# A three-block transformer pass: the fourth mixer's latent query scaling, a key turn and four insertions moved

## The chip, the cores and the metric

One NeuronCore of a Trainium2 chip runs the whole program in one launch. Its engines work side by side and meet only by semaphores: PE multiplies matrices, DVE (vector) and ACT (scalar) work on elements, POOL (GpSimd) does a few small ones, SP issues the DMAs. The metric is the device time of one execution in microseconds; the kernel before takes 1460.8 us (median of 3 runs, 1460.72 to 1460.99).

## The reference

256 rows of 1024 features pass through two layers of a first block (feed-forward, mixer, feed-forward), then one layer of a second block. The "fourth mixer" of this text is the mixer of the second block. It runs two attentions of 8 heads beside each other, "fox" with forget gates and "latent" (MLA), and adds them under sigmoid gates:

```
proj = h @ w_in[l]
(q_lat, kv_lat, k_rope, fq, fk, fv, f_logit, g_mla, g_fox) = jnp.split(proj, split_points, axis=-1)
y_mla = mla_mixer(q_lat, kv_lat, k_rope, cos, sin, ...)   # q, k: 64 normalised + 32 rotated columns
y_fox = fox_mixer(fq, fk, fv, f_logit, ...)               # q, k: 64 normalised columns, decay from f_logit
mixed = (jax.nn.sigmoid(g_mla + b_gate[l, 0]) * (y_mla @ w_branch_mla[l])
         + jax.nn.sigmoid(g_fox + b_gate[l, 1]) * (y_fox @ w_branch_fox[l]))
x = x + mixed @ w_o[l]
```

In `mla_mixer` the queries come from `rms_norm(q_lat) @ w_qb`. Each head's 64 plain and 32 rotary columns are normalised apart, and the rotary ones are then rotated by position. The rotated key (32 columns, from `k_rope`) is the same for all heads. Both attentions are causal softmax(q k) v.

## The kernel before, in words

Every float32 weight matrix is streamed from HBM and multiplied in three passes. The weights lie in blocks of at most 512 rows by 512 columns (1 MB), in the order of the list `plan`. For each block SP loads it into one of 4 slots of `raw`; ACT casts it to a high part `whi` (line 1193); DVE subtracts to get a low part `wlo` (line 1632); PE multiplies high by high, low by high and high by low (lines 563 to 565). `whi` and `wlo` have 3 slots each. A cast waits until PE is done with the block three places before, a load until DVE has made the low part of the block four places before. In the programs of ACT and DVE `unit()` is the cast or the low part of the next block; both run a few blocks ahead of PE.

`steps(job, i, j0, j1)` is PE's work on row tiles j0 to j1 of block i of a job: per row tile two halves of the rows and three matmuls each. A full block has 4 row tiles, 24 matmuls. Before each matmul group it waits for the low part of the block:

```
q.wait_ge(*s_dve[job.key, kt])
q.wait_ge(*s_lo[v, j])
```

In the mixers these blocks are one piece each: `s_lo` is raised once, when the whole low part is done.

Each engine's program is one list, written out by hand and executed in order. PE's list sets insertions between `steps` of the gate blocks (`gate2[0]` to `gate2[3]`, each with two blocks, 0 and 1): the attention's transposes, scores and values, which need results of ACT, DVE and POOL. PE's PSUM is handed out as 4 pairs of banks in a ring (`take`, `give`); a pair comes free when ACT or DVE has read it.

The insertions, of PE unless named otherwise:

- `fox_turn(g)`: transposes of 4 heads of fox queries and keys (line 1018); ACT copies them to `mQT`, `mKT` (line 1480).
- `fox_scores(g)`: matmuls q k of 4 heads (line 717). DVE's `logits` adds the causal mask and takes maxima (lines 1893, 1896), ACT's `softmax` the exponentials (line 1324), DVE's `normalise` divides (lines 1904, 1906).
- `probabilities(mat, ("f", g), g)`: transposes of the probabilities (lines 730 to 736), copied by ACT (line 1336) and DVE (line 1914).
- `fox_values(g)`: matmuls p v (lines 750, 751), read out by `turned` on ACT and DVE.
- `rope_key_turn()`: two transposes of the rotated key, which POOL makes (lines 2342 to 2260, `s_pool["kr", 1]`); ACT copies it to all heads (line 1549).
- `mla_queries(g)`, `mla_keys()`, `mla_scores(g)`: the same for the latent attention (lines 1010, 1018, 717; ACT lines 1486, 1492).

The latent queries' norm factors come from DVE's `head_factors("q")`; `head_scale("q")` multiplies them in, 4 instructions (line 2106). Then POOL rotates the rotary columns (lines 2349, 2258, 2260), and PE's `mla_queries(0)` waits for that (`s_pool["qrope", 1]`).

In DVE's list the order around the change is: low part of `kvb[1]` (512 columns, small); `head_scale("q")`; low part of `gate2[0]`, block 1; logits of both fox groups; `normalise` of the first; low part of `gate2[1]`, block 0; copy of probabilities; `gate(0)`; `normalise` of the second; low part of `gate2[1]`, block 1. In ACT's list the copy of the rotated key stands behind the cast of `gate2[3]`, block 0.

Of the kernel before, what the change touches and what calls it, by code (L numbers as in the profile page):

```python
# [183 lines left out]
def bc(ap, dim, n):  # L184
    a = ap.unsqueeze(dim)
    shape = list(a.shape)
    shape[dim] = n
    return a.broadcast_to(shape)


def program(nc, T, out):
    with ExitStack() as ctx:
# [341 lines left out]
        def tensor(e):  # L534
            q = Waits(e)
            idle = [(0, ()), (1, ()), (2, ()), (3, ())]

            def take(name):
                i, emptied = idle.pop(0)
                for mark in emptied:  # L540
                    q.wait_ge(*mark)
                pair_of[name] = i
                return Pair(name)

            def give(name, *emptied):
                idle.append((pair_of[name], emptied))

            def steps(job, i, j0=0, j1=4):
                v = job.at[i]
                k0, nk, _ = job.blocks[i]  # L550
                pair = take(job.name) if i == 0 and j0 == 0 else Pair(job.name)
                wd, end = job.width, i == len(job.blocks) - 1
                order = [(j, tt) for j in range(j0, min(j1, nk)) for tt in range(2)]
                if v == len(plan) - 1:
                    return last_steps(job, pair, v, k0, nk)
                for j, tt in order:
                    kt, n = k0 // 128 + j + job.k_off, job.rows(i, j)
                    q.wait_ge(*s_dve[job.key, kt])
                    q.wait_ge(*s_lo[v, j])
                    hi_w, lo_w = (w[0:n, v % SPLIT, j * wd:(j + 1) * wd] for w in (whi, wlo))  # L560
                    h, l = (a[0:n, kt, 128 * tt:128 * tt + 128] for a in (job.act.hi, job.act.lo))
                    o = pair.ap[:, tt, 0:wd]
                    e.matmul(o, h, hi_w, start=i == 0 and j == 0, stop=False)  # L563
                    e.matmul(o, h, lo_w, start=False, stop=False)  # L564
                    t = e.matmul(o, l, hi_w, start=False, stop=(end or (v == len(plan) - 2 and tt == 1)) and j == nk - 1)  # L565
                    if j == nk - 1:
                        t.then_inc(s_mm.mark((v, tt), *([(job.name, tt)] if end else [])), 1)

            def last_steps(job, pair, v, k0, nk):

                wd, own = job.width, take("last")
                for tt, c0, n in ((0, 0, wd), (1, 0, wd // 2), (1, wd // 2, wd // 2)):
                    o = own.ap[:, c0 // (wd // 2), 0:n] if tt else pair.ap[:, 0, :]
                    for j in range(nk):
                        kt = k0 // 128 + j + job.k_off
                        q.wait_ge(*s_dve[job.key, kt])
                        q.wait_ge(*s_lo[v, j])
                        hi_w, lo_w = (w[:, v % SPLIT, j * wd + c0:j * wd + c0 + n] for w in (whi, wlo))
                        h, l = (a[:, kt, 128 * tt:128 * tt + 128] for a in (job.act.hi, job.act.lo))
                        e.matmul(o, h, hi_w, start=tt == 1 and j == 0, stop=False)  # L580
                        e.matmul(o, h, lo_w, start=False, stop=False)
                        t = e.matmul(o, l, hi_w, start=False, stop=j == nk - 1)
                    names = [("last", tt, c0)]
                    if c0 + n == wd:
                        names += [(v, tt), (job.name, tt)]
                    t.then_inc(s_mm.mark(*names), 1)
# [407 lines left out]
            def mla():  # L994
# [26 lines left out]
                def fox_turn(g):  # L1021
                    pair = take(("fx", g))
                    q.wait_ge(*s_pool["hn", "fq"])
                    two_heads(pair, 0, ("fxq", g), FQ, g)
                    q.wait_ge(*s_dve["hn", "fk"])
                    two_heads(pair, 1, ("fxk", g), FK, g)
                    give(("fx", g), s_act["fxk", g])
# [7 lines left out]
                def fox_values(g):  # L1035
                    q.wait_ge(*s_act["fv"])
                    values(mat, ("f", g), lambda h, st: FV[:, st, 64 * (4 * g + h):64 * (4 * g + h) + 64], 64, ("yt", "fox"), 4 + 2 * g)

                def rope_key_turn():
                    pair = take("krt")  # L1040
                    q.wait_ge(*s_pool["kr", 1])
                    for tt in range(2):
                        t = e.transpose(pair.ap[0:96, 0, 128 * tt:128 * tt + 128], KR[:, tt, :], ident[:, :])
                    t.then_inc(s_turn.mark("krt"), 1)
                    give("krt", s_act["krt"])
# [42 lines left out]
                steps(kvb[0], 0)  # L1088
                give(kvb[0].name, s_act["kv", 0])
                fox_turn(0)  # L1090
                steps(gate2[0], 0, 0, 2)
                fox_turn(1)
                steps(gate2[0], 0, 2, 3)
                fox_scores(0)
                steps(gate2[0], 0, 3)
                fox_scores(1)
# [3 lines left out]
                probabilities(mat, ("f", 0), 0)  # L1100
                give(gate2[0].name, s_dve["gate", 0])
                steps(gate2[1], 0)
                fox_values(0)
                steps(gate2[1], 1, 0, 2)
                probabilities(mat, ("f", 1), 1)
                steps(gate2[1], 1, 2, 3)
                fox_values(1)
                steps(gate2[1], 1, 3)
                give(gate2[1].name, s_dve["gate", 1])
                steps(gate2[2], 0, 0, 1)  # L1110
                rope_key_turn()
                mla_queries(0)
                mla_keys()
                steps(gate2[2], 0, 1, 3)
# [58 lines left out]
            ffn(b2)  # L1173
            ffn(c1)
            mla()
            ffn(c2)

        def scalar(e):
            q = Waits(e)
            at_unit = [0]  # L1180

            def unit():
                v = at_unit[0]
                at_unit[0] += 1
                if v < len(plan):
                    for js, n, c in pieces(v):
                        high(v, js, n, c)
# [274 lines left out]
            def mla():  # L1462
# [20 lines left out]
                def mla_queries(g):  # L1483
                    q.wait_ge(*s_turn["m_", "s", ("f", 1), 0])
                    q.wait_ge(*s_turn["mq", g])
                    e.mul(mQT[:, 4 * g:4 * g + 4, :], Pair(("mq", g)).flat[0:96, :].rearrange("p (h t) -> p h t", h=4),
                          96.0 ** -0.5).then_inc(s_act.mark(("mq", g)), 1)
# [55 lines left out]
                probabilities(mat, ("f", 1), ("f", 0))  # L1543
                unit()
                turned(("m_", "v", ("f", 1)), YT, 6, None, (128,) * 2)
                unit()
                q.wait_ge(*s_turn["m_", "s", ("f", 1), 0])
                q.wait_ge(*s_turn["krt"])
                e.copy(mKT[64:96, :, :], bc(Pair("krt").ap[64:96, 0, 0:256], 1, 8)).then_inc(s_act.mark("krt"), 1)
                mla_queries(0)  # L1550
                mla_keys(0)
                mla_keys(1)
# [57 lines left out]
        def vector(e):  # L1610
            q = Waits(e)
# [3 lines left out]
            def after_mine():  # L1615
                q.wait_ge(*s_dve.now())

            def unit():
                v = at_unit[0]
                at_unit[0] += 1  # L1620
                if v < len(plan):
                    ps_ = pieces(v)
                    for p in ps_:
                        low(v, *p, done=p is ps_[-1])
# [274 lines left out]
            def normalise(at, g, i):  # L1899
                name = at.name  # L1900
                for tt in (1, 0):
                    L, c = at.part(i, tt)
                    q.wait_ge(*s_act[name, "exp", g, tt])
                    e.reciprocal(at.ri[:, c:c + 4], at.sm[:, c:c + 4]).then_inc(s_dve.mark(), 1)
                    after_mine()
                    e.tensor_tensor(L, L, at.ri[:, c:c + 4].unsqueeze(2).broadcast_to([128, 4, 128 * (tt + 1)]),
                                    ALU.mult).then_inc(s_dve.mark((name, "P", g, tt)), 1)
# [173 lines left out]
            def mla():  # L2081
# [20 lines left out]
                def head_scale(name):  # L2102
                    views = norm_views[name]
                    after_mine()
                    for i, x in enumerate(views):
                        t = e.tensor_tensor(x, x, r24[:, 8 * i:8 * i + 8].unsqueeze(2).broadcast_to([128, 8, x.shape[2]]), ALU.mult)
                        t.then_inc(s_dve.mark(*([("hn", name)] if i == len(views) - 1 else [])), 1)
# [44 lines left out]
                head_sums("q", (2, 3))  # L2152
                head_factors("q")
                unit()
                head_scale("q")
                unit()
                logits(mat, ("f", 0), 0, causal)
                logits(mat, ("f", 1), 1, causal, ("fxk", 1))
                normalise(mat, ("f", 0), 0)
                unit()  # L2160
                q.wait_ge(*s_pool["kr", 1])
                probabilities(mat, ("f", 0))
# [250 lines left out]
```

## Time and profile before

| | |
|---|---|
| median of 3 runs | 1460.8 us (1460.72 to 1460.99) |
| span of the profiled execution, first to last instruction | 1458.9 us |
| PE busy | 1452.6 us |
| DVE, ACT, POOL busy | 1002.6, 778.5, 87.2 us |
| all waits of PE for another engine | 3.4 us |

The span is the profiled execution's own time. It leaves out what lies before the first and behind the last instruction, so it stands 1.9 us below the runs' median. Times inside it are in us from its start; the fourth mixer lies at about 1110 to 1290. A row of a timeline gives start, duration, engine, line, operation, output and inputs, and count, and in brackets the idle time ahead of it with the engine that ended it. Matmul ends are modelled and overlap, so PE's rows are read by their starts.

### The profile page before, as it was taken

To read this page: it belongs to the slowest core of one execution; us is meant where nothing else is said; L and a number is where in the kernel's file an instruction comes from. 1 tells how busy PE (TensorE), PEld (TensorE's weight loads), DVE (VectorE), ACT (ScalarE), POOL (GpSimd) and SP (SyncE) were. 2 spreads that over 40 slices of the span, in tenths; PEclk is the share of its full clock that TensorE was granted. 3 is DMA by queue.
4 is the path that set the end of the run, shared out by engine and by line. 5 is a ranking of instruction groups with operands and counts; after the bars stand their busy time and mean duration, and the time that the engine had idled before them with its cause. 6 is when DMAs were issued, how large, how long until landed. Compare 5 with 4: busy or idle time off the path is not lost.

```text
span 1458.9 us, 18627 instructions
## 1 busy us (share of the span) xinstructions
PE 1452.6 (100%) x7822; PEld 1250.3 (86%) x7822; DVE 1002.6 (69%) x1216; ACT 778.5 (53%) x971; POOL 87.2 (6%) x113
## 2 busy tenths in 40 slices
PE   9999999999999999999999999999999999999999
PEld 7888888888888888888888888888888888888887
DVE  6976466787755867459877664787646987687653
ACT  6654355655534555345665544564435876465542
POOL 0000003000000000006100000000000800000000
PEclk9999999999999999999999999999999999999999
DMA  9855563556556555545455556475556543556552
GB/s 328 277 183 178 160 203 116 168 180 201 179 182 202 187 187 189 186 139 172 150 198 188 189 172 206 154 223 182 187 173 217 188 144 118 173 193 205 178 187 72
DMA packets 205620, 266.82 MB, mean 183 GB/s; under 512 B 6944, under 2 KB 148880, under 8 KB 205280
## 3 DMA queue, kind: packets, MB, share of 16 engines
q1 hardware_dynamic: 204320, 261.23, 54.5%
q0 software_dynamic: 1072, 4.35, 0.8%
q8 instruction: 62, 1.02, 0.3%
q14 instruction: 22, 0.18, 0.0%
q10 hardware_dynamic: 144, 0.05, 0.0%
HBM read 264.56 MB, written 1.05 MB: 182 GB/s over the span
## 4 chain that ended last, share of the span: by engine, by line
PE 96%; DVE 2%; ACT 1%; DMA 0%; issue 0%; DVEq 0%; ACTq 0%
PE ps L637 33%; PE ps L643 17%; PE ps L563 14%; PE ps L565 13%; PE ps L564 13%; PE ps L616 1%; PE ps L717 1%; PE ps L812 1%; DVE wlo L1632 1%; PE ps L750 1%; DVE d_i L2025 0%; DVE d_m L2021 0%; DMA G<-in_gains 0%; DVE d_i L2049 0%; PE ps L751 0%
## 5 line engine op out<-in xcount | busy, mean ns | idle before, releaser
L1632 DVE TENSOR_TENSOR wlo<-raw,whi 128x2048 fp32r<-128x2048 f32 (+5 forms) x275 | 567.4, 2068 | 259.0 <-ACT whi L1193 258.6
L1193 ACT CAST whi<-raw 128x2048 fp32r<-128x2048 f32 (+5 forms) x275 | 474.7, 1732 | 222.8 <-PE ps L565 218.4
L637 PE MATMUL ps<-xt,whi 128*128 128x512 f32 x2112 | 511.2, 391 | 0.5 <-DVE xt L2225 0.5
L637 PEld LDWEIGHTS ps<-xt,whi 128*128 128x128 f32 x2112 | 386.0, 188 | 74.4 <-DVE xt L2225 1.3
L643 PEld LDWEIGHTS ps<-xt,wlo 128*128 128x128 f32 x2112 | 274.0, 191 | 12.3
L643 PE MATMUL ps<-xt,wlo 128*128 128x256 f32 x2112 | 277.7, 283 | 0.0
L563 PE MATMUL ps<-whi,xt 128*128 128x512 f32 (+4 forms) x304 | 112.7, 371 | 0.0
L565 PE MATMUL ps<-whi,xt 128*128 128x512 f32 (+4 forms) x304 | 109.7, 361 | 0.0
L564 PE MATMUL ps<-wlo,xt 128*128 128x512 f32 (+4 forms) x304 | 109.5, 360 | 0.0
L563 PEld LDWEIGHTS ps<-whi,xt 128*128 128x128 f32 x304 | 57.3, 188 | 9.2 <-issue 1.0
L565 PEld LDWEIGHTS ps<-whi,xt 128*128 128x128 f32 x304 | 57.2, 188 | 8.5
L564 PEld LDWEIGHTS ps<-wlo,xt 128*128 128x128 f32 x304 | 57.4, 189 | 7.4
L1206 ACT ACTIVATE xt<-ps,G 128x256 fp32r<-128x256 f32 x64 | 25.1, 474 | 35.6 <-PE ps L616 35.5
L563 PE MATMUL ps<-whi,yt_hi 128*128 128x512 f32 (+3 forms) x108 | 42.7, 395 | 0.0
L565 PE MATMUL ps<-whi,yt_lo 128*128 128x512 f32 (+3 forms) x108 | 41.7, 386 | 0.0
L564 PE MATMUL ps<-wlo,yt_hi 128*128 128x512 f32 (+3 forms) x108 | 41.6, 386 | 0.0
L1222 ACT ACTIVATE junk<-X 128x512 f32<-128x512 f32 x40 | 25.4, 634 | 28.5 <-DVE X L1690 27.3
L1646 DVE SCALAR_TENSOR_TENSOR xt<-ps,G,xt 128x256 fp32r<-128x256 f32 x64 | 26.5, 477 | 15.6 <-ACT xt L1206 15.6
L563 PE MATMUL ps<-whi,a1ht_hi 128*128 128x512 f32 x88 | 34.3, 390 | 0.0
L563 PE MATMUL ps<-whi,a2ht_hi 128*128 128x512 f32 x88 | 34.3, 390 | 0.0
L563 PE MATMUL ps<-whi,b1ht_hi 128*128 128x512 f32 x88 | 34.3, 390 | 0.0
L563 PE MATMUL ps<-whi,b2ht_hi 128*128 128x512 f32 x88 | 34.3, 390 | 0.0
(422 smaller groups left out, 1885.8 us busy)
## 6 DMA issues: line engine op xcount, KB each, us to landing
raw<-in_ffn_wi SPq DMA_DIRECT2D x85, 1024.0 KB, 4.9
raw<-in_ffn_wo SPq DMA_DIRECT2D x40, 1024.0 KB, 5.0
raw<-in_ffn_w_gate SPq DMA_DIRECT2D x22, 1024.0 KB, 5.1
raw<-in_ffn_w_up SPq DMA_DIRECT2D x22, 1024.0 KB, 5.2
raw<-in_ffn_w_down SPq DMA_DIRECT2D x20, 1024.0 KB, 4.9
raw<-in_w_in SPq DMA_DIRECT2D x14, 1024.0 KB, 5.1
raw<-in_even_w_in SPq DMA_DIRECT2D x6, 1024.0 KB, 5.2
raw<-in_ffn_wo SPq DMA_DIRECT2D x8, 512.0 KB, 3.8
```

Source lines behind the costliest of these rows:

```text
L563: e.matmul(o, h, hi_w, start=i == 0 and j == 0, stop=False)
L564: e.matmul(o, h, lo_w, start=False, stop=False)
L565: t = e.matmul(o, l, hi_w, start=False, stop=(end or (v == len(plan) - 2 and tt == 1)) and j == nk - 1)
L616: t = e.transpose(pair.flat[0:n, 256 * b + 128 * tt:256 * b + 128 * tt + 128], halves[tt], ident[:, :])
L637: return e.matmul(pair.ap[:, b, :], whi[:, v % SPLIT, 256 * j + 128 * b:256 * j + 128 * b + 128], XS[:, j, :, :].rearrange("p h t -> p (h ...
L643: e.matmul(pair.ap[:, b, 0:256], wlo[:, v % SPLIT, 256 * j + 128 * b:256 * j + 128 * b + 128], XS[:, j, 0, :], start=False, stop=False)
L717: t = e.matmul(pair.flat[:, w * h:w * h + w], queries(h)[0:n, 128 * tt:128 * tt + 128], keys(h)[0:n, 0:w], start=True, stop=True)
L1193: e.copy(whi[0:n, v % SPLIT, c], raw[0:n, v % RAW, c]).then_inc(s_hi.mark(*[(v, j) for j in js]), 1)
L1206: t = e.mul(act.hi[0:n, kt0 + i, :], pair.flat[0:n, 256 * i:256 * i + 256], 1.0 if gains is None else gains(i)[0:n, :])
L1222: e.activation(junk[:, :], X[:, tt, 512 * n:512 * n + 512], ACT.Square, accum_out=ssq[:, tt, n:n + 1]).then_inc(s_act.mark(("sq", x, n, tt ...
L1632: e.tensor_tensor(wlo[0:n, v % SPLIT, c], raw[0:n, v % RAW, c], whi[0:n, v % SPLIT, c].bitcast(F32), ALU.subtract).then_inc(s_lo.mark(*[(v ...
L1646: t = e.scalar_tensor_tensor(l, src, gains(i)[0:n, :], h.bitcast(F32), ALU.mult, ALU.subtract)
```

## The change

Four moves, in the programs of PE, ACT and DVE; no instruction is added or taken away.

- PE: the second fox turn follows the first directly, and the first three row tiles of `gate2[0]`, block 0, come behind both.
- PE: one row tile of `gate2[1]`, block 1, comes ahead of the first fox values, which are then followed directly by the second fox probabilities; the next two row tiles come behind these.
- PE and ACT: the rotated key's turn moves from `gate2[2]` to behind the second fox values, and ACT's copy of it to before the cast of `gate2[3]`, block 0.
- DVE: `head_scale("q")` moves from ahead of the low part of `gate2[0]`, block 1, to behind `normalise` of the first fox group.

```diff
@@ tensor, mla
                 fox_turn(0)
-                steps(gate2[0], 0, 0, 2)
                 fox_turn(1)
-                steps(gate2[0], 0, 2, 3)
+                steps(gate2[0], 0, 0, 3)
                 fox_scores(0)
                 steps(gate2[0], 0, 3)
                 fox_scores(1)
...
                 steps(gate2[1], 0)
+                steps(gate2[1], 1, 0, 1)
                 fox_values(0)
-                steps(gate2[1], 1, 0, 2)
                 probabilities(mat, ("f", 1), 1)
-                steps(gate2[1], 1, 2, 3)
+                steps(gate2[1], 1, 1, 3)
                 fox_values(1)
+                rope_key_turn()
                 steps(gate2[1], 1, 3)
                 give(gate2[1].name, s_dve["gate", 1])
                 steps(gate2[2], 0, 0, 1)
-                rope_key_turn()
                 mla_queries(0)
@@ scalar, mla
                 turned(("m_", "v", ("f", 1)), YT, 6, None, (128,) * 2)
-                unit()
                 q.wait_ge(*s_turn["m_", "s", ("f", 1), 0])
                 q.wait_ge(*s_turn["krt"])
                 e.copy(mKT[64:96, :, :], bc(Pair("krt").ap[64:96, 0, 0:256], 1, 8)).then_inc(s_act.mark("krt"), 1)
+                unit()
                 mla_queries(0)
@@ vector, mla
                 head_factors("q")
                 unit()
-                head_scale("q")
                 unit()
                 logits(mat, ("f", 0), 0, causal)
                 logits(mat, ("f", 1), 1, causal, ("fxk", 1))
                 normalise(mat, ("f", 0), 0)
+                head_scale("q")
                 unit()
```

## Rows read from the trace of the kernel before

**Rows 1.** The page, busy time by engine (us, share, instructions).
```profile
PE 1452.6 (100%) x7822; PEld 1250.3 (86%) x7822; DVE 1002.6 (69%) x1216; ACT 778.5 (53%) x971; POOL 87.2 (6%) x113
```
**Rows 2.** PE's waits, whole span: total us, times, longest.
```profile
...
PE ps L717 <- DVE m_L L1893: 0.7, 1, 0.7
...
PE ps L717 <- ACT m_kt L1492: 0.2, 1, 0.2
```
**Rows 3.** The chain of waits, 1157 to 1197 us: start, us, what.
```profile
1157.53 2.06 DVE m_qf L2106 x4
...
1191.83 1.87 ACT m_kt L1549
...
1195.33 0.70 ACT m_kt L1492
```
**Rows 4.** DVE's timeline, 1157 to 1199 us.
```profile
1157.44 2.14 DVE L2106 TENSOR_TENSOR m_qf<-m_qf,m_r 128x512 f32<-128x512 f32 x4
1159.51 2.30 DVE L1632 TENSOR_TENSOR wlo<-raw,whi 128x2048 fp32r<-128x2048 f32 x1
1161.73 1.21 DVE L1893 SCALAR_TENSOR_TENSOR m_L<-causal,ps 128x1024 f32<-128x1024 f32 x1
...
1171.28 2.28 DVE L1632 TENSOR_TENSOR wlo<-raw,whi 128x2048 fp32r<-128x2048 f32 x1
...
1177.56 2.29 DVE L1632 TENSOR_TENSOR wlo<-raw,whi 128x2048 fp32r<-128x2048 f32 x1
...
1198.10 1.22 DVE L1893 SCALAR_TENSOR_TENSOR m_L<-causal,ps 128x1024 f32<-128x1024 f32 x1 [2.45 <-PE ps L717]
```
**Rows 5.** ACT's timeline, 1151 to 1192 us.
```profile
1151.17 1.27 ACT L1230 ACTIVATE m_fv<-ps,RS 128x512 f32<-128x512 f32 x2 [0.76 <-PE ps L565]
...
1156.19 2.42 ACT L1193 CAST whi<-raw 128x512 fp32r<-128x512 f32 x2
...
1159.86 1.38 ACT L1480 ACTIVATE m_kt<-ps,G 64x512 f32<-64x512 f32 x2
...
1189.89 1.92 ACT L1193 CAST whi<-raw 128x2048 fp32r<-128x2048 f32 x1 [0.98 <-PE ps L565]
```
**Rows 6.** PE's timeline, 1158 to 1197 us.
```profile
1158.21 2.78 PE L717 MATMUL ps<-m_kt,m_qt 80*128 80x256 f32 x16
...
1163.08 2.86 PE L717 MATMUL ps<-m_kt,m_qt 80*128 80x256 f32 x16 [0.70 <-DVE m_L L1893]
...
1173.82 0.48 PE L563 MATMUL ps<-whi,xt 128*128 128x512 f32 x1
...
1179.16 0.39 PE L565 MATMUL ps<-whi,xt 128*128 128x512 f32 x1
1179.48 0.66 PE L750 MATMUL ps<-m_P,m_fv 128*64 128x256 f32 x4
...
1180.98 0.50 PE L563 MATMUL ps<-whi,xt 128*128 128x512 f32 x1
...
1195.49 0.39 PE L565 MATMUL ps<-whi,xt 128*128 128x512 f32 x1
1196.07 2.88 PE L717 MATMUL ps<-m_kt,m_qt 96*128 96x256 f32 x16 [0.19 <-ACT m_kt L1492]
```
**Rows 7.** POOL's timeline, 1140 to 1170 us.
```profile
1140.36 2.71 POOL L2335 TENSOR_SCALAR m_qt<-m_c,m_fc 16x256 f32<-16x256 f32 x1
...
1149.27 0.55 POOL L2335 TENSOR_SCALAR m_qt<-m_c,m_fc 16x256 f32<-16x256 f32 x1
...
1162.55 0.72 POOL L2349 TENSOR_TENSOR m_qf<-m_qf,m_rg 128x256 f32<-128x256 f32 x1
...
1168.63 0.74 POOL L2260 TENSOR_TENSOR m_qf<-m_lat 128x256 f32<-128x256 f32 x1
```
**Rows 8.** Instructions of DVE line 2106: count, ns min/median/max, first and last start.
```profile
L2106 DVE TENSOR_TENSOR m_fk<-m_fk,m_r x2: 678/804/931, 1146.1 to 1147.0; 128x512 f32<-128x512 f32 x2
```
**Rows 9.** The page, DMA issues: KB each, us to landing.
```profile
raw<-in_w_in SPq DMA_DIRECT2D x14, 1024.0 KB, 5.1
```

## The prediction, on record before the result

> **What bounds the kernel now.** The page's first part comes first: PE is busy for 1452.6 of 1458.9 us, so only PE's gaps can be won or lost [rows 1]. PE's own waits come next. Of its few, two lie in the fourth mixer: the second fox scores wait 0.70 us for a logits instruction of DVE, the first latent scores 0.2 us for a key copy of ACT [rows 2]. The chain of waits around the two says why. Ahead of the fox scores stand `head_scale("q")`, a low part and the logits, all on DVE; ahead of the latent scores stands a row of ACT copies with the rotated key's among them [rows 3]. After that the stretch was read engine by engine, in the timelines.
>
> The latent wait is longer than its row, if one goes by starts: the last gate matmul ahead of it starts at 1195.49, and they come every 0.23 (24 of a block from 1173.82 to 1179.16, 23 steps), so the scores could start at 1195.72 and start at 1196.07: 0.35 lost [rows 6].
>
> What is as near to the path, but leaves no wait in the trace, is the low part of a gate block. That of `gate2[1]`, block 0, runs on DVE from 1171.28 for 2.28 and ends at 1173.56; PE starts the block at 1173.82 [rows 4, 6]. From the end of the logits at 1161.73 + 1.21 = 1162.94 to the start of PE that waited for it, at 1163.08, a signal takes 0.14, so this low part is 0.12 early. The next one, of block 1, ends at 1179.85, for PE 1179.99. PE starts that block at 1180.98, but only because the fox values lie ahead of it from 1179.48. At the end of block 0, 1179.16 + 0.23 = 1179.39, it would have come too late by 0.6 [rows 4, 6].
>
> **The change part by part.**
>
> *`head_scale("q")` behind the first logits.* Ahead of the logits its place closes, but not by its length. DVE now goes straight from the small low part to that of `gate2[0]`, block 1, and its cast ends on ACT at 1156.19 + 2.42 = 1158.61. ACT works without a gap from 1151.17 to there (five rows), so this can't come sooner [rows 5]. With the 0.14 the low part starts at 1158.75 instead of 1159.51, and with its 2.22 to the next start the logits begin at 1160.97 instead of 1161.73: 0.76 earlier, out of 2.07 taken away (1157.44 to 1159.51) [rows 4]. The scores that they read come 2.03 after their start (the latent ones: 1196.07 to DVE's 1198.10 [rows 4, 6]); 1158.21 + 2.03 = 1160.24 is early enough. PE's second fox scores start at 1160.97 + 1.21 + 0.14 = 1162.32: **-0.76**. ACT's second fox copies, which they need as well, end at 1161.24 as before [rows 5]. PE itself is free by 1163.08 - 0.70 = 1162.38 at the latest.
>
> Behind the logits the whole length comes back. The twelve rows of DVE from 1161.73 to 1171.28 have no idle time, so `normalise` of the first group leaves DVE at 1170.52, `head_scale` at 1172.59; the low part of `gate2[1]`, block 0, ends at 1172.59 + 2.28 = 1174.87, for PE 1175.01. PE, 0.76 earlier, asks for it at 1173.06. `steps` waits for the low part before its first matmul, and the block has one piece, so nothing of it can start: **+1.95**. Behind that wait all of PE's list is queued.
>
> *The row tile put ahead of the first fox values.* PE is through block 0 in 5.57 (1173.82 to 1179.39), at 1180.58. Block 1's first row tile now comes at once, without the values as its cover. DVE starts that low part 6.28 after the one before (1171.28 to 1177.56): 1178.87, done at 1181.16, for PE 1181.30. A second wait, of 0.72. To this comes POOL. It takes up the latent queries' rotations (1162.55 to 1169.37, 6.8 us [rows 7]) only when `head_scale` is done, from some 1172.6 on, beside three DVE instructions that decide this wait: `normalise` of the second group (two multiplications) and the low part. Below nothing it can't go, since the three run with POOL idle today. Above, if each waited out one POOL instruction of 0.74 [rows 7], 2.2. The nearest row is `head_scale` of the fox keys, two instructions of one form, of which one took 0.93 beside POOL and one 0.68 [rows 8]: 0.25 lost by one in two. I take 0.2, nearer to that row: **+0.92** with the 0.72.
>
> On this place the Trainium skill speaks against the change. The trace: a POOL instruction that ran into a low part took 2.71, its like later 0.55 [rows 7]. SBUF — State Buffer, section "Who interferes with whom", says that a Vector instruction with two SBUF inputs and a GpSimd instruction that reads SBUF exclude each other for a whole instruction, and the one that starts first goes first. The trace agrees for POOL as the one that waits; DVE's 0.25 is far from a whole instruction. By the rule the sum would have 2.2 in place of 0.2, by the row it has 0.2.
>
> *The key turn after the second fox values.* Its two transposes are moved, not added: 0 on PE. POOL makes its keys ahead of the query rotations of 1162.55, long before. On ACT its copy of 1.87 leaves the chain of cast, copy, query copy and key copies that ends at 1196.03 and holds the latent scores [rows 3]. It now stands ahead of the cast of `gate2[3]`, block 0, partly in the idle 0.98 before it [rows 5]. With PE 2.0 late there (-0.76 + 1.95 + 0.92 - 0.1), ACT is done with the copies ahead of the cast at 1189.89 - 0.98 + 2.0 = 1190.9, with the key's copy (1.87) at 1192.8, with the cast (1.92) at 1194.7 and, after the 2.33 that now lie from the end of the key's copy at 1193.70 to that of the first key copies at 1196.03 [rows 3], at 1197.0; PE asks for them at 1195.72 + 2.0 = 1197.7. So the lost 0.35 goes: **-0.35**. That cast is some 0.7 later for it, and its low part is wanted only after the latent logits, for which DVE waits 2.45 anyway [rows 4]. If the cover of 0.7 were gone, the 0.35 would stay.
>
> *The joined pairs.* Fox turn with fox turn, values with probabilities, and values with the key turn: two interruptions of the gate matmuls fewer. Going in, the first values start 0.09 late (1179.39 to 1179.48 [rows 6]); with as much going out, two interruptions are worth at most 0.4, and 0 if the transposes beside give it back. I take **-0.1**, nearer to that single row.
>
> What else moves. The four PSUM pairs go round in the old order but for one swap: the second fox turn takes the pair that the second query copy freed, the gate block the one that the value copy frees at 1151.17 + 1.27. The query copy stands earlier in ACT's list, and the gate block is first wanted behind both turns, at some 1153.9; neither waits. A load starts when the low part four blocks before is done: behind that of `gate2[1]`, block 0 (1174.87 now), that is the load of `gate2[3]`, block 0, which takes 5.1 [rows 9] and is cast at 1189.89 or later. The rotations, if three low parts of 2.29 shut POOL out in full, end at 1172.6 + 6.8 + 6.9 = 1186.3; PE turns the queries at about 1193.
>
> **Sum:** -0.76 + 1.95 + 0.92 - 0.35 - 0.1 = +1.7 us. Behind the mixer PE has no wait in which a late start could vanish, so it goes to the end: span 1460.6. The span is 1.9 below the runs' median of 1460.8; with the same around it, **1462.5 us**. About 0.2%, 2.9 us, is what a measurement of this kernel tells from no change.
>
> **The rivals.**
>
> A. *Only the first low part is late* (1461.5). Block 1's is covered, if DVE makes up 0.7 between the two. For it: what DVE reads there from PE and ACT comes 0.8 earlier now. Against: it doesn't wait for these today, so there is nothing to shorten. The sum without the 0.92.
>
> B. *DVE waits out POOL's rotations* (1464.5). Three DVE instructions at 0.74, 2.2 instead of 0.2. For: POOL's 2.71 shows that the two hold each other up. Against: DVE's own rows, with 0.25 lost in two. It decides once a rotation is running whenever DVE comes to `normalise` or the low part. That is what the Trainium skill's section named above would have.
>
> C. *No low part is late: faster than before* (1459.6). Then only -0.76, -0.35 and -0.1 are left. It decides if the low part of `gate2[1]`, block 0, is done by 1172.9, 1.95 earlier than in my chain. For: the chain of waits does name `head_scale` among what holds the scores, and from there it goes. Against: logits can't start before their scores, 1160.24, which gives 0.73 at most, and the rest would need shorter logits; they took 1.21 with POOL beside them and 1.22 without [rows 4].
>
> **How the numbers follow.** My forecast 0.68 (its own range 1461.5 to 1463.5, from the joins' 0.4 and DVE's 0 to 1), A 0.12, B 0.10, C 0.10. The range from 1459.8 to 1464.1 holds the forecast, A and part of B. Slower by over 0.2% needs 1463.7: most of B and the forecast's tail, 0.10. Faster by over 0.2% needs 1457.9, below C: 0.02. Between them 0.88.
>
> **What would show it.** Among PE's waits: the fox scores' nearly gone; a new one of some 1.9 of a gate matmul (L563) on a low part (L1632) behind the first fox probabilities, a second of 0.7 to 1 at the next block; none at the latent scores. On DVE: logits 0.8 earlier, four instructions of L2106 directly ahead of a low part of 2.3, no idle between. On POOL: the rotations after 1172, stretched beside low parts, done by 1188. The forecast is wrong if PE starts `gate2[1]` on time, if the query turn waits for POOL, or if the granted clock leaves 1.00 in this stretch.

## The result and the profile after

The changed kernel takes 1463.1 us (median, 1462.79 to 1463.49), the kernel before in the same runs 1460.84: 1.0015 of it, interval 1.0009 to 1.0022. That is 2.26 us more, where 1.7 more was forecast; 1463.1 lies in the range 1459.8 to 1464.1. It is below the 0.2% that the prediction took as what can be told from no change; with the 20 runs of either the interval is narrow enough to call it slower, by a little.

PE's work is the same, its waits are not. The page's first part and PE's waits of the changed kernel (total us, times, longest), to be set beside [rows 1, 2]:

```profile
PE 1452.6 (99%) x7822; PEld 1250.2 (86%) x7822; DVE 1004.2 (69%) x1216; ACT 778.2 (53%) x971; POOL 91.5 (6%) x113
```

```profile
PE ps L563 <- DVE wlo L1631: 3.3, 2, 1.7
PE ps L1159 <- DVE junk L2219: 1.5, 1, 1.5
PE ps L730 <- DVE d_L L1905: 0.5, 1, 0.5
PE ps L637 <- DVE xt L2224: 0.2, 1, 0.2
```

Both waits of the scores (L717) are gone; two waits of gate matmuls for a low part have come, 3.3 us. (One line of the code is gone, so the later lines count one less, some two.) PE's timeline of the changed kernel, beside [rows 6]:

```profile
1157.93 2.78 PE L717 MATMUL ps<-m_kt,m_qt 80*128 80x256 f32 x16
...
1161.96 2.85 PE L717 MATMUL ps<-m_kt,m_qt 80*128 80x256 f32 x16
...
1174.58 0.47 PE L563 MATMUL ps<-whi,xt 128*128 128x512 f32 x1 [1.60 <-DVE wlo L1631]
...
1179.43 0.39 PE L563 MATMUL ps<-whi,xt 128*128 128x512 f32 x1
...
1181.94 0.50 PE L563 MATMUL ps<-whi,xt 128*128 128x512 f32 x1 [1.67 <-DVE wlo L1631]
...
1198.27 2.78 PE L717 MATMUL ps<-m_kt,m_qt 96*128 96x256 f32 x16
1200.89 1.04 PE L1010 MATMUL ps<-ident,m_qf 128*96 128x128 f32 x8
```

Read by starts, the stretch from the first fox scores to the first latent ones is 40.34 us long (1157.93 to 1198.27) and was 37.86 (1158.21 to 1196.07 [rows 6]): 2.48 more, by three parts. First to second fox scores: 4.03 against 4.87. From there to gate2[1], block 0: 12.62 against 10.74. From there to the latent scores: 23.69 against 22.25. These ran 0.10 shorter themselves (2.62 against 2.72 to the query turn behind them). They no longer start out of a wait, and in none of the eight experiments below do they: there they ran 2.61 to 2.67.

DVE's timeline of the changed kernel says where the two waits come from, beside [rows 4]:

```profile
1158.39 2.29 DVE L1631 TENSOR_TENSOR wlo<-raw,whi 128x2048 fp32r<-128x2048 f32 x1 [1.11 <-ACT whi L1192]
1160.60 1.21 DVE L1892 SCALAR_TENSOR_TENSOR m_L<-causal,ps 128x1024 f32<-128x1024 f32 x1
...
1170.27 1.96 DVE L2105 TENSOR_TENSOR m_qf<-m_qf,m_r 128x512 f32<-128x512 f32 x4
1172.15 2.28 DVE L1631 TENSOR_TENSOR wlo<-raw,whi 128x2048 fp32r<-128x2048 f32 x1
...
1176.47 1.52 DVE L1905 TENSOR_TENSOR m_fq<-m_fq,m_ri 128x1024 f32<-128x1024 f32 x1
1177.91 0.17 DVE L1903 RECIPROCAL m_ri<-m_sm 128x4 f32<-128x4 f32 x1
1178.11 1.03 DVE L1905 TENSOR_TENSOR m_fk<-m_fk,m_ri 128x512 f32<-128x512 f32 x1
1179.06 2.82 DVE L1631 TENSOR_TENSOR wlo<-raw,whi 128x2048 fp32r<-128x2048 f32 x1
```

The time that `head_scale` used to fill ahead of the logits is now 1.11 us of idle before a low part, and the 1.96 that it takes lies directly ahead of the low part that PE waits for first. The two multiplications of `normalise` and the second low part took 1.52, 1.03 and 2.82. In the kernel before the low part took 2.29 [rows 4], and the two multiplications (DVE's timeline):

```profile
1175.60 1.23 DVE L1906 TENSOR_TENSOR m_fq<-m_fq,m_ri 128x1024 f32<-128x1024 f32 x1
...
1176.95 0.69 DVE L1906 TENSOR_TENSOR m_fk<-m_fk,m_ri 128x512 f32<-128x512 f32 x1
```

POOL's timeline of the changed kernel shows what stood beside them ([rows 7] are the same rotations before):

```profile
1172.31 2.72 POOL L2348 TENSOR_TENSOR m_qf<-m_qf,m_rg 128x256 f32<-128x256 f32 x1 [11.03 <-DVE m_qf L2105]
1175.17 1.74 POOL L2257 TENSOR_TENSOR m_lat<-m_qf,trig 128x128 f32<-128x128 f32 x4
1176.98 1.60 POOL L2259 TENSOR_TENSOR m_qf<-m_lat 128x256 f32<-128x256 f32 x1
1178.67 1.07 POOL L2348 TENSOR_TENSOR m_qf<-m_qf,m_rg 128x256 f32<-128x256 f32 x1
```

The first, 0.72 before, is held for nearly the whole low part of block 0; the next ones fall on `normalise` and the second low part, and both engines lose.

### The profile page after: what moved, and what is told of

It reads as the page before. It is cut to its first block, busy times and chain, and to the rows that moved or that the text cites. A ratio compares the mean times of both kernels' runs of the same rounds, so it can differ in the third digit from the quotient of the medians.

```text
span 1461.1 us, 18628 instructions
## 1 busy us (share of the span) xinstructions
PE 1452.6 (99%) x7822; PEld 1250.2 (86%) x7822; DVE 1004.2 (69%) x1216; ACT 778.2 (53%) x971; POOL 91.5 (6%) x113
## 4 chain that ended last, share of the span: by engine, by line
PE 95%; DVE 3%; ACT 1%; issue 0%; DMA 0%; DVEq 0%
PE ps L637 33%; PE ps L643 17%; PE ps L563 13%; PE ps L565 13%; PE ps L564 13%; PE ps L616 1%; DVE wlo L1631 1%; PE ps L812 1%; PE ps L717 1%; PE ps L750 1%; DVE d_i L2024 0%; DVE d_m L2020 0%; DVE d_i L2048 0%; DMA G<-in_gains 0%; DVE m_nm L1895 0%
## 5 line engine op out<-in xcount | busy, mean ns | idle before, releaser
L2257 POOL TENSOR_TENSOR d_tmp<-d_k,trig 128x128 f32<-128x128 f32 x8 | 8.7, 1117 | 412.8 <-ACT d_k L1229 412.8
```

## The experiments

The theory put to the test: PE loses because DVE's work now falls between the wrong low parts, and because POOL's rotations stretch that work. The rivals: PE's new order loses the time, or POOL costs DVE nothing. All times below are medians beside runs of the kernel before on the same chip (1460.85 for the first four, 1460.76 for the last four).

**Only `head_scale` moved.**

```diff
 (the kernel before, vector)
-                head_scale("q")
                 unit()
                 logits(mat, ("f", 0), 0, causal)
                 logits(mat, ("f", 1), 1, causal, ("fxk", 1))
                 normalise(mat, ("f", 0), 0)
+                head_scale("q")
```

> Only DVE's head_scale("q") is moved; PE and ACT keep the order of before. My theory (the late low parts carry the loss): the fox scores' wait on DVE goes, PE then waits some 1.6 us for the low part of gate2[1], block 0, net +1.0 us at that block's start; block 1, with the fox values ahead of it again, waits only 0.2 us, although its low part and the normalise ahead of it are stretched by POOL as in the changed kernel (2.8 us instead of 2.3); the latent scores' wait of 0.2 stays. 1462.0 us, +1.2. The rival, that PE's new order loses the time: between -0.8 and 0, 1460.0 to 1460.8.

Measured: 1462.63 us, 1.0012 (1.0003 to 1.0021). The one moved line carries 1.8 of the 2.26 us; the rival is out. It is 0.6 above my number, and PE's waits and the two rows behind them in this kernel's PE timeline show why:

```profile
PE ps L563 <- DVE wlo L1632: 2.0, 2, 1.6
...
PE ps L750 <- DVE m_P L1914: 0.3, 1, 0.3
```

```profile
1174.68 0.47 PE L563 MATMUL ps<-whi,xt 128*128 128x512 f32 x1 [1.64 <-DVE wlo L1632]
...
1188.10 0.66 PE L750 MATMUL ps<-m_P,m_fv 128*64 128x256 f32 x4 [0.34 <-DVE m_P L1914]
...
1191.54 0.50 PE L563 MATMUL ps<-whi,xt 128*128 128x512 f32 x1 [0.32 <-DVE wlo L1632]
```

With the values ahead of it, block 1 doesn't wait at all. But DVE's lateness is still there and meets PE later: at the second fox values, for DVE's copy of the probabilities, and at gate2[2]. By starts the two cost 0.61 and 0.58, more than the idle time in their rows, and the 0.35 of the latent scores goes, since PE comes to them later: 0.84 in all, where I had 0.2. I had followed DVE's list to block 1 only.

**All but `head_scale`.** The changed kernel with DVE's line put back.

```diff
 (the changed kernel, vector)
                 unit()
+                head_scale("q")
                 unit()
...
                 normalise(mat, ("f", 0), 0)
-                head_scale("q")
```

> PE's and ACT's moves alone; head_scale("q") stays where it was. My theory: the fox scores wait 0.7 us for DVE as before, gate2[1], block 0, doesn't wait, block 1's first row tile comes 0.6 us ahead of its low part and waits for that, the latent scores' 0.35 us goes, the joined pairs give 0.1. Sum +0.15 us, 1461.0. The rival, PE's new order: +1.5 to +2.3 us, 1462.3 to 1463.1.

Measured: 1460.87 us, 1.0000 (0.9991 to 1.0009). PE's order loses nothing in sum. The row tile ahead of the values waits 0.35 by its row and 0.51 by starts (0.6 was expected), the latent scores don't (PE's timeline of this kernel):

```profile
1163.11 2.86 PE L717 MATMUL ps<-m_kt,m_qt 80*128 80x256 f32 x16 [0.74 <-DVE m_L L1892]
...
1179.93 0.50 PE L563 MATMUL ps<-whi,xt 128*128 128x512 f32 x1 [0.35 <-DVE wlo L1631]
...
1196.25 2.78 PE L717 MATMUL ps<-m_kt,m_qt 96*128 96x256 f32 x16
```

**The values first again.**

```diff
 (the changed kernel, tensor)
-                steps(gate2[1], 1, 0, 1)
                 fox_values(0)
+                steps(gate2[1], 1, 0, 2)
                 probabilities(mat, ("f", 1), 1)
-                steps(gate2[1], 1, 1, 3)
+                steps(gate2[1], 1, 2, 3)
```

> The changed kernel with one part undone: the first fox values stand ahead of gate2[1], block 1, again, and the second fox probabilities behind two of its row tiles. My theory: the first wait on a low part (1.6 us) stays, the second (1.67 us) shrinks to 0.2 us, since the values take 1.5 us of PE that it would else idle; 1461.65 us, 1.45 below the changed kernel. The rival, that block 1 is late by POOL whatever stands ahead of it: PE's wait moves and doesn't shrink, 1463.1.

Measured: 1462.43 us, 1.0011 (1.0002 to 1.0020); 0.67 below the changed kernel's median and not 1.45. The second wait goes, against the rival, but two waits come at the places that the first experiment found, the second fox values and `gate2[2]` (PE's timeline of this kernel):

```profile
1188.37 0.66 PE L750 MATMUL ps<-m_P,m_fv 128*64 128x256 f32 x4 [0.32 <-DVE m_P L1913]
...
1191.81 0.50 PE L563 MATMUL ps<-whi,xt 128*128 128x512 f32 x1 [0.15 <-DVE wlo L1631]
```

By starts they cost 1.01: from the first fox values to the latent scores PE takes 17.22 here (1180.60 to 1197.82) and 16.21 in the kernel of "The key turn and two joins" below (1179.59 to 1195.80), whose PE list is the same and which has no wait there. So of the 1.83 won at block 1 some 0.8 is left in this trace.

**The rotations later.**

```diff
 (the changed kernel, gpsimd)
                 q.wait_ge(*s_dve["hn", "q"])
+                q.wait_ge(*s_lo[gate2[1].at[1], "all"])
```

> The changed kernel, but POOL takes up the query rotations only when the low part of gate2[1], block 1, is done. If POOL beside DVE lengthens normalise and that low part (by 0.29, 0.34 and 0.53 us in the changed kernel's trace), they return to 1.23, 0.69 and 2.29 us and PE's second wait falls from 1.67 to 0.5 us: 1461.95 us, 1.15 less; the rotations end by 1190 and PE's query turn at some 1192.6 doesn't wait. If POOL costs DVE nothing and the order of DVE's list alone makes the second wait, the time stays 1463.1. If the rotations come too late, PE waits at the query turn and the time is above 1463.

Measured: 1462.67 us, 1.0013 (1.0004 to 1.0022). DVE's timeline of this kernel:

```profile
1176.57 1.22 DVE L1905 TENSOR_TENSOR m_fq<-m_fq,m_ri 128x1024 f32<-128x1024 f32 x1
...
1177.92 0.69 DVE L1905 TENSOR_TENSOR m_fk<-m_fk,m_ri 128x512 f32<-128x512 f32 x1
1178.53 2.29 DVE L1631 TENSOR_TENSOR wlo<-raw,whi 128x2048 fp32r<-128x2048 f32 x1
...
1182.03 0.36 DVE L1656 TENSOR_SCALAR nv<-m_s 128x8 f32<-128x8 f32 x2
...
1183.82 0.59 DVE L1667 SCALAR_TENSOR_TENSOR ny<-nb,ny 128x16 f32<-128x16 f32 x1
...
1186.99 0.74 DVE L1643 TENSOR_TENSOR yt_lo<-ps,yt_hi 128x256 fp32r<-128x256 f32 x2
```

The three rows are back at 1.22, 0.69 and 2.29, and PE's second wait is 0.46: POOL was the rest of it. But the time falls by 0.4 only, not 1.15. The rotations now run beside the small instructions of `head_factors` for the latent keys, which take 4.96 (1182.03 to 1186.99) where they took 2.67 in the kernel before (1181.07 to 1183.74, DVE's timeline):

```profile
1181.07 0.25 DVE L1657 TENSOR_SCALAR nv<-m_s 128x8 f32<-128x8 f32 x2
...
1183.74 0.75 DVE L1644 TENSOR_TENSOR yt_lo<-ps,yt_hi 128x256 fp32r<-128x256 f32 x2
```

PE waits 0.21 and 0.15 at the second values and `gate2[2]`. By starts that is 0.68: from block 1 to the latent scores PE takes 17.01 here (1180.87 to 1197.88) and 16.33 in the changed kernel (1181.94 to 1198.27). POOL's price was not taken away, it was put on other DVE work.

**POOL alone.** The reverse test, on the kernel before:

```diff
 (the kernel before, gpsimd)
                 q.wait_ge(*s_dve["hn", "q"])
+                q.wait_ge(*s_dve["m_", "P", ("f", 0), 0])
```

> The kernel before, with DVE's, ACT's and PE's lists untouched; POOL alone takes up the query rotations only when DVE has normalised the first fox group, so that they run beside the low parts of gate2[1] as in the changed kernel. If POOL beside DVE is what lengthens normalise and the low part, their rows are 1.5, 1.0 and 2.8 us here too instead of 1.23, 0.69 and 2.29; DVE then is 1.1 us late at block 1's low part, of which PE has 1.0 to spare, and PE waits 0.1 to 0.2 us there and 0.1 to 0.4 us at the second fox values and the next block: 1461.2 to 1461.5 us. If POOL costs DVE nothing, the rows and the time are those of before, 1460.8.

Measured: 1461.45 us, 0.7 above the kernel before (1.0005, 0.9996 to 1.0013: the ranges of the single runs, 1461.1 to 1461.7 and 1460.35 to 1461.05, don't meet). DVE's timeline of this kernel, with DVE's list untouched:

```profile
1175.82 1.50 DVE L1906 TENSOR_TENSOR m_fq<-m_fq,m_ri 128x1024 f32<-128x1024 f32 x1
...
1177.44 1.02 DVE L1906 TENSOR_TENSOR m_fk<-m_fk,m_ri 128x512 f32<-128x512 f32 x1
1178.39 2.83 DVE L1632 TENSOR_TENSOR wlo<-raw,whi 128x2048 fp32r<-128x2048 f32 x1
```

The same three lengths as in the changed kernel, from POOL's place alone. PE waits 0.34 at the second values and 0.31 at `gate2[2]`; at block 1, where I had 0.1 to 0.2, it doesn't wait.

**The key turn and two joins.** The second experiment's kernel with the values first.

```diff
 (the changed kernel, tensor, then vector)
-                steps(gate2[1], 1, 0, 1)
                 fox_values(0)
+                steps(gate2[1], 1, 0, 2)
                 probabilities(mat, ("f", 1), 1)
-                steps(gate2[1], 1, 1, 3)
+                steps(gate2[1], 1, 2, 3)
...
                 head_factors("q")
                 unit()
+                head_scale("q")
                 unit()
...
                 normalise(mat, ("f", 0), 0)
-                head_scale("q")
```

> The key turn's move and the two joins that need no row tile moved: before, with both fox turns together, the key turn behind the second fox values, and ACT's copy of it ahead of the cast. The fox scores wait 0.7 us as before, no low part is late, the latent scores' wait goes: -0.35 for it and up to -0.1 for the joins, 1460.4 us. The rival, that the copy ahead of the cast delays the latent query copies as much as it frees them: 1460.8.

Measured: 1460.20 us, 0.56 below before (0.9996, 0.9987 to 1.0005; single runs 1460.03 to 1460.47). The interval takes in no change, and the single runs overlap with those of before, so the time alone doesn't settle it. In the trace no low part is late and the latent scores don't wait (PE's timeline of this kernel):

```profile
1195.80 2.78 PE L717 MATMUL ps<-m_kt,m_qt 96*128 96x256 f32 x16
```

From the first fox scores to the query turn behind the latent ones PE takes 40.13 (1158.28 to 1198.41), and 40.58 in the kernel before (1158.21 to 1198.79): 0.45 less, what these parts were said to be worth.

**`head_scale` split in two ways**, on that kernel:

```diff
 (vector; the first way has [2, 3, 0] and [1], the second [2, 3] and [0, 1])
                 unit()
-                head_scale("q")
+                head_scale("q", [2, 3])
                 unit()
                 logits(mat, ("f", 0), 0, causal)
...
                 head_scale("k")
                 unit()
+                head_scale("q", [0, 1], ("hn", "q plain"))
                 turned(("m_", "v", ("f", 1)), ("yt", "fox"), YT, 6, None, (128,) * 2)
```

`mla_queries` waits for the late mark too, and the key factors go to columns 16 to 31 of `r24`.

> head_scale("q") split: both rotary parts and the first plain part stay ahead of the logits, in the 1.1 us in which DVE has nothing to do but wait for ACT's cast; the second plain part (0.65 us) goes behind the low part of gate2[2], block 0, where DVE waits for ACT anyway. The factors of the latent keys are written beside those of the queries for that, and the query turn waits for the late part too. PE has the moves of the change but for the row tile ahead of the first fox values. My theory (what counts is where DVE's work falls between low parts, and POOL may not rotate beside them): logits 0.5 us earlier, no low part late, rotations beside the logits as before and DVE's rows at 1.23, 0.69 and 2.29; -0.5 at the fox scores, -0.35 at the latent ones, -0.1 for the joins: 1459.9 us. The rival, that any work of head_scale behind the logits comes back on PE: above 1460.5.

> As the split 3 and 1, but only the two rotary parts stay ahead of the logits (0.8 us of the 1.1 us that DVE waits there) and both plain parts (1.3 us) go behind the low part of gate2[2], block 0. The fox scores' wait goes in full (-0.8), the latent scores' too (-0.35), joins -0.1: 1459.55 us, if the gate sum behind the plain parts still frees its PSUM pair before the latent key turn wants it (1191.4 against 1191.3 by my count); if not, that turn waits some 0.1 to 0.3 us. The rival as there: above 1460.5.

Measured: 1459.65 (0.9993, 0.9984 to 1.0002) and 1459.40 us (0.9991, 0.9983 to 1.0000). The second beats both kernels: 1.36 us below before and 3.7 below the change, all its runs (1459.17 to 1459.72) under all of before's, though the interval reaches 1.0000. The rival is out for both: no run of either is above 1460.1. In its PE waits none is left in the fourth mixer, and on DVE the moved work lies where nothing waits for it (PE's waits, then DVE's timeline):

```profile
PE ps L1160 <- DVE junk L2224: 1.5, 1, 1.5
PE ps L637 <- DVE xt L2229: 0.7, 1, 0.7
PE ps L730 <- DVE d_L L1906: 0.5, 1, 0.5
```

```profile
1157.18 0.86 DVE L2109 TENSOR_TENSOR m_qf<-m_qf,m_r 128x256 f32<-128x256 f32 x2
1158.38 2.29 DVE L1632 TENSOR_TENSOR wlo<-raw,whi 128x2048 fp32r<-128x2048 f32 x1 [0.34 <-ACT whi L1193]
...
1176.54 2.28 DVE L1632 TENSOR_TENSOR wlo<-raw,whi 128x2048 fp32r<-128x2048 f32 x1
...
1187.51 1.28 DVE L2109 TENSOR_TENSOR m_qf<-m_qf,m_r 128x512 f32<-128x512 f32 x2
```

The rotary parts use most of the wait for ACT's cast, so POOL rotates beside the logits as before; the plain parts come after the last low part that PE wants soon.

## Why the prediction was right, and where a size was off

| step | forecast | by the traces |
|---|---|---|
| second fox scores | -0.76 | -0.84 (4.03 against 4.87) |
| first low part late | +1.95 | +1.88 (12.62 against 10.74) |
| second low part late | +0.92 | +1.83 |
| latent scores | -0.35 | -0.45 (0.35 of wait, and 0.10 that they ran shorter) |
| joined pairs | -0.1 | -0.04, what is left over in this stretch |

*`head_scale` behind the first logits.* Right in mechanism and in both sizes. The length came back in full (1.96) ahead of the low part, and only 0.84 of it had been won, since ACT's cast holds DVE for 1.11 of the rest. The first experiment shows that this one line alone loses 1.8.

*The row tile ahead of the first fox values.* The mis-sized term. After block 0 PE was free at 1179.43 + 3 x 0.23 = 1180.11 and started at 1181.94: 1.83. Of the 0.92, the 0.72 from DVE's order stands (0.66 by starts with the rotations held off: block 0 from 1174.68, as long as here, and block 1 at 1180.87). The failing step is "I take 0.2" for POOL: it was 0.29 + 0.34 + 0.53 = 1.16. The row that I went by [rows 8] had 0.25 lost by one of two instructions, and I put about that for three; taken for each of the three it would have been 0.75. Rival B, with 0.74 each, had 2.2: on this term it was as far off as I was, to the other side.

On the rule of SBUF — State Buffer, section "Who interferes with whom", in the Trainium skill: the trace agrees that both sides wait, DVE too, and not only POOL, as I had it. But a whole POOL instruction for each of the three, the price that the prediction gave the rule, is not what the rows show. Each side waited out what was left of the instruction that the other had running. The POOL rows from 1175.17, 1176.98 and 1178.67 end at 1176.91, 1178.58 and 1179.74; that is 0.44, 0.47 and 0.68 behind the starts of the three DVE instructions (1176.47, 1178.11, 1179.06), and these lost 0.29, 0.34 and 0.53, each 0.13 to 0.15 less. The low part from 1172.15 ends 2.12 behind POOL's start at 1172.31, and POOL lost 2.00. In the kernel of "POOL alone" the three DVE instructions started 0.42, 0.48 and 0.67 ahead of the ends of POOL's rows (1176.24, 1177.92, 1179.06), and lost 0.27, 0.33 and 0.54. The row that I took for a measure of POOL's price says the same (the kernel before, POOL's timeline, then DVE's):

```profile
1145.95 0.56 POOL L2337 TENSOR_SCALAR m_kt<-m_c,m_fc 16x256 f32<-16x256 f32 x1
```

```profile
1146.12 1.53 DVE L2106 TENSOR_TENSOR m_fk<-m_fk,m_r 128x512 f32<-128x512 f32 x2
```

This POOL row ends at 1146.51, 0.39 behind DVE's start, and DVE lost 0.25 [rows 8]. So the 0.25 was no fixed price: it came from where DVE's start happened to fall in POOL's instruction, and it didn't speak against B's mechanism, as the prediction had it. B's mechanism holds; its price, a whole instruction each time, was too high.

*The key turn* and *the joined pairs.* Right. The latent wait is gone, with 0.10 more because the scores ran shorter without a wait ahead of them (1198.27 to 1200.89, 2.62; before, 1196.07 to the query turn at 1198.79, 2.72). The joins are near nothing. In the kernel with these two alone the stretch is 0.45 shorter.

*The rivals.* A is out: the second low part is late. C is out: the low part came 1.9 late, as the chain said. In the sum the terms give 2.48 less the 0.10, and the runs 2.26.

*What the prediction did not see:* that past the second low part DVE's list stays as tight. It did not matter here, because the second wait set PE back behind it; it showed as soon as an experiment took that wait away, and cost three of my expectations 0.6 to 0.8 us (in the experiment with the rotations later, together with POOL's new place).

## What to carry to other kernels

On an engine that runs its list in order, moving work to directly ahead of a producer that the bottleneck is about to wait for cost nearly its full length there (1.88 of 1.96), and won at its old place only what nothing else held up (0.84). A producer that lands 0.12 us early shows no wait in a profile; put its end beside its consumer's start before something is placed ahead of it. What paid here was to split such work, with the part that a third engine waits for in an idle stretch and the rest behind the last urgent producer. And when two engines hold each other up, the price is what is left of the other's running instruction when one starts, so read it from starts and ends and not from one row's loss.

## What the runs showed of the hardware

What POOL's rotations and DVE cost each other depended on what DVE was running. Beside `normalise` and the low parts both lost: POOL's 0.72 became 2.72 beside a low part, DVE's 1.23, 0.69 and 2.29 became 1.52, 1.03 and 2.82, and what was lost is the rest of the other's running instruction less 0.12 to 0.15. Beside fourteen small instructions of 8 and 16 columns only DVE lost: these took 4.96 instead of 2.67 in all, while POOL's multiplications took 0.74 and 0.76. Beside the logits, which read PSUM and the mask, neither lost: DVE's took 1.21 in the kernel before with POOL at work and 1.22 without [rows 4], POOL's 0.72 to 0.75. That the small ones lose most, 2.29 in all where the three large ones lost 1.16, I had not expected.
